# RWKV's core in joint steps of both head pairs, w and a beside attention's end, a gate that overlaps its units: one core, 2432 dense rows

## The reference, cut to what matters

```python
def first_block(x, p, ...):
    h = rmsnorm(x, norm_mix_g[i]);  u = h @ w_in[i]
    u_rwkv, u_attn, u_gate = jnp.split(u, ...)
    o_a = rwkv7_time_mix(u_rwkv, ...)      # 8 heads of 64; w, a, g through small matrices w2, a2, g2
    o_b = diff_attention(u_attn, ...)      # 4 heads, two causal score matrices each, rmsnorm of the output
    g_a, g_b = jnp.split(jax.nn.sigmoid(u_gate), 2, axis=-1)
    merged = g_a * (o_a @ w_proj_a[i]) + g_b * (o_b @ w_proj_b[i])
    x = x + merged @ w_out[i]
    x = x + jnp.square(jax.nn.relu(rmsnorm(x, norm_mlp_g[i]) @ w_ff1[i])) @ w_ff2[i]
    gate = jax.nn.sigmoid(rmsnorm(x, norm_ple_g[i]) @ w_ple_gate[i])
    x = x + (p[i] @ w_ple[i]) * gate       # the first gate of the texts below
    return rmsnorm(x, final_norm_g)
def second_block(x, p, ...):
    # h = rmsnorm(x, ln1) @ w_in: gated linear attention (GLA, 4 heads) and dilated attention
    # (12 heads in 3 groups, mixed by a softmax over the groups' lse), both gated;
    # then w_out, the same MLP, a second gate, the last norm
```

## Time and profile before

| | |
|---|---|
| median of 3 runs | 2204.41 us (2203.53 to 2207.41) |
| profiled execution | 2209.3 us, its span 2207.5 us |
| TensorE busy | 2107.3 us (95%), 11518 matmuls, mean granted clock 0.967 |
| VectorE, ScalarE, GpSimd busy | 979.0 us (44%), 791.4 us (36%), 316.7 us (14%) |
| DMA | 84 GB/s in the mean, 173 MB read from HBM |

### The profile page before, as it was taken

How to read it: one execution, slowest core, us unless ns; L and a number is a source line. 1 busy time by engine, 2 the same in 40 slices (tenths; PEclk the granted TensorE clock), 3 DMA queues, 4 the chain that set the end, 5 groups by cost and what they waited for, 6 DMA issues and landing times.

```text
span 2207.5 us, 27571 instructions
## 1 busy us (share of the span) xinstructions
PE 2107.3 (95%) x11518; PEld 1651.1 (75%) x11518; DVE 979.0 (44%) x1510; ACT 791.4 (36%) x1241; POOL 316.7 (14%) x314
## 2 busy tenths in 40 slices
PE   7889999999999999999889999999899999999996
PEld 5556766767788778888666778888588888888884
DVE  5554454444463233336644344444744442333354
ACT  5445212221445332234642233334332343322344
POOL 2001122121122010012500000000401120100114
PEclk9989998989999999999999999999999999999998
DMA  4112111111442332323231112222132333222221
GB/s 167 48 48 67 49 45 39 46 43 45 148 138 96 105 103 97 100 93 103 94 106 48 48 66 68 81 83 86 48 105 96 99 104 131 96 96 96 96 86 48
DMA packets 59845, 185.47 MB, mean 84 GB/s; under 512 B 6552, under 2 KB 11800, under 8 KB 59593
## 3 DMA queue, kind: packets, MB, share of 16 engines
q1 hardware_dynamic: 59720, 183.71, 24.9%
HBM read 173.46 MB, written 10.22 MB: 83 GB/s over the span
## 4 chain that ended last, share of the span: by engine, by line
PE 85%; DVE 4%; ACT 3%; issue 3%; POOL 3%; DMA 1%; SPq 0%; DVEq 0%; POOLq 0%; ACTq 0%
PE P L493 24%; PE P L495 22%; PE P L494 22%; POOL AREN L2287 1%; POOL AREN L2290 1%; PE P L778 1%; DVE AREN L1615 1%; PE P L794 1%; PE P L787 1%; PE P L845 1%; PE P L844 1%; PE P L933 1%; PE P L735 1%; ACT WHI L1052 1%; PE P L981 1%
## 5 line engine op out<-in xcount | busy, mean ns | idle before, releaser
L493 PE MATMUL P<-HH,WHI 128*128 128x512 f32 x1528 | 651.0, 426 | 19.5 <-DVE WLO L1622 13.9
L495 PE MATMUL P<-HH,WLO 128*128 128x512 f32 x1528 | 608.5, 398 | 0.0
L494 PE MATMUL P<-HL,WHI 128*128 128x512 f32 x1528 | 607.8, 398 | 0.0
L1052 ACT ACTIVATE WHI<-RAW 128x1024 fp32r<-128x1024 f32 x303 | 318.7, 1053 | 395.0 <-PE P L495 392.4
L1622 DVE TENSOR_TENSOR WLO<-RAW,WHI 128x1024 fp32r<-128x1024 f32 x303 | 381.3, 1259 | 155.5 <-ACT WHI L1052 154.1
L493 PEld LDWEIGHTS P<-HH,WHI 128*128 128x128 f32 x1528 | 293.1, 192 | 112.4 <-issue 31.7
L493 PE MATMUL P<-ARR,WHI 128*128 128x512 f32 (+1 forms) x904 | 353.6, 391 | 11.0 <-DVE WLO L1622 7.4
L495 PE MATMUL P<-ARR,WLO 128*128 128x512 f32 (+1 forms) x904 | 352.1, 390 | 0.0
L494 PE MATMUL P<-ARR,WHI 128*128 128x512 f32 (+1 forms) x904 | 352.0, 389 | 0.0
L495 PEld LDWEIGHTS P<-HH,WLO 128*128 128x128 f32 x1528 | 293.8, 192 | 64.8
L494 PEld LDWEIGHTS P<-HL,WHI 128*128 128x128 f32 x1528 | 294.6, 193 | 49.7 <-issue 1.2
(11 more groups left out here) (289 smaller groups left out, 1613.1 us busy)
## 6 DMA issues: line engine op xcount, KB each, us to landing
RAW<-in_w_in_dram SPq DMA_DIRECT2D x118, 512.0 KB, 3.3
RAW<-in_w_ff_dram SPq DMA_DIRECT2D x64, 512.0 KB, 3.3
RAW<-in_w_ml_dram SPq DMA_DIRECT2D x64, 512.0 KB, 3.3
RAW<-in_w_out_dram SPq DMA_DIRECT2D x16, 512.0 KB, 3.3
RAW<-in_w_pg_dram SPq DMA_DIRECT2D x16, 512.0 KB, 3.2
AREN<-in_xT_dram SPq DMA_DIRECT2D x16, 256.0 KB, 6.3
s_gates<-AREN SPq DMA_DIRECT2D x16, 256.0 KB, 2.0
RAW<-in_w_ab_dram SPq DMA_DIRECT2D x8, 512.0 KB, 3.3
```

The costliest lines, as they stand in the source:

```text
L493: e.matmul(out, hi, H[0][:, s], start=first, stop=False)
L494: e.matmul(out, hi, H[1][:, s], start=False, stop=False)
L495: return e.matmul(out, lo, H[0][:, s], start=False, stop=last)
L1052: e.activation(WHI[n % NSPL][:, :], RAW[n % NRAW][:, :], ACT.Copy).then_inc(*D.act.sig("whi", n))
```

## The change

`gate_steps` places the six steps of a unit over two units. `n5` is no longer squared by ScalarE and added by GpSimd: VectorE sums the squares of `n4`, weighted with `GF2` (g_fin squared, formed once). The norm totals stand in rows EMB2 + 8, EMB2 + 14 and HA, and the eight products x by one each in every fourth row of GL.

`attn_steps` lists attention's 64 steps for all engines; several share a row, and `pv` and `ss` of a head stand between the scores of the next one. The steps of w and a (`r`) move from rows 132 to 147 to rows 117 to 131 and into banks 6 and 7. The area of w's and a's results is moved to the end of the buffers, and w2 is loaded into a buffer of pair 1 without a wait; g2 waits for the last head's `bia` (the ALiBi table).

`core_steps` lists 70 steps of a pair: `la` of level 1 also holds the a and v transposes, level 2 the mean, level 4 the variance, level 5 the gate of the quarter before, level 3 the bonus; `lb` holds `lb`, `lc` and in level 5 `x1`; W holds b's transposes, N a state. Each step has its fixed banks. Both pairs take their steps in the same rows, 21 steps of pair 0 ahead, at every second row from 164 on. `yw` and `yb` of GpSimd become two `scalar_tensor_tensor` of VectorE in `result`. Only the last quarter has three steps `E` of its own.

GLA's and the dilated heads' steps share rows (15 steps of a GLA head in 10 rows), the mix takes four rows (HR + 50 to 62) of three steps, with banks 4 to 7.

```diff
 def gate_steps(j, k, n):
 
-    stages = ("evac", "sigmoid", "mult", "add", "hi", "lo")
-    out = [(j, "evac")] if 2 <= j < n and k == 7 else []
-    if j == 2:
-        out = [(i, stages[k - 1 - i]) for i in range(2) if 0 <= k - 1 - i < 6] + out
-    if j > 2 and 1 <= k <= 5:
-        out.append((j - 1, stages[k]))
+
+    out = []
+    for i in range(n):
+        if i == 0:
+            at = (2, 1), (2, 2), (2, 3), (2, 6), (3, 0), (3, 1)
+        elif i == 1:
+            at = (2, 2), (2, 3), (2, 4), (3, 0), (3, 3), (3, 5)
+        elif i < n - 1:
+            at = (i, 7), (i + 1, 1), (i + 1, 2), (i + 1, 6), (i + 2, 0), (i + 2, 1)
+        else:
+            at = (i, 7), (n, 1), (n, 2), (n, 3), (n, 4), (n, 5)
+        out += [(i, what) for what, jk in zip(("evac", "sigmoid", "mult", "add", "hi", "lo"), at) if jk == (j, k)]
     return out
...
+def attn_steps():
+    out = []
+    for h in range(4):
+        out += [("vt", 0, 0)] if h == 0 else []
+        for i in range(8):
+            out += [("pv", h - 1, 0)] if h and i == 1 else [("ss", h - 1, 0)] if h and i == 5 else []
+            out.append(("qk", h, i))
+        out.append(("aw", h, 0))
+        out += [("vt", h + 1, 0)] if h < 3 else []
+        out += [("pt", h, kb) for kb in (3, 2, 1, 0)]
+    out += [("pv", 3, 0), ("ss", 3, 0)]
+    banked = [s for s in out if s[0] != "aw"]
+    return [(*s, (2, 3, 4, 5)[banked.index(s) % 4] if s[0] != "aw" else None) for s in out]
+def core_steps():
+    out = []
+    for q in range(4):
+        out += [("G", q, 0), ("T", q, 0)]
+        for lev in range(1, 6):
+            out += [("la", q, lev), ("lb", q, lev)]
+        out += [("W", q, 0), ("M", q, 0), ("N", q, 0)] + ([("S", q, 0)] if q < 3 else []) + [("O", q, 0)]
+    return out + [("E", 3, i) for i in range(3)]
...
-    def spread(seq, first, last):
-        for i, s in enumerate(seq):
-            at[first + i * (last - first) // len(seq)].append(s)
-
-    for h in range(4):
-        r = (33, 57, 81, 105)[h]
-        put("a", r, *range(r + 3, r + 11), r + 13, *range(r + 17, r + 21), r + 22, r + 24)
-    put("r", 132, *range(136, 144), 147)
-    for jj, first, last in ((0, A_RW + 68, A_GA + 124), (1, A_GA + 4, A_GA + 126)):
-        c, f = f"c{jj}", f"f{jj}"
-        seq = [f, f, f]
-        for q in range(4):
-            more = [f] if q < 3 else []
-            seq += [c] * 8 + more + [c] * 17 + more + [c] * 2 + more + [c] * (5 if q < 3 else 4)
-        spread(seq, first, last)
-    put("n", A_EMB2 + 7, A_EMB2 + 11, A_EMB2 + 13, A_EMB2 + 15)
+    put("a", 32)
+    for r in (39, 62, 85, 108):
+        late = r > 39
+        put("a", r, r, *((r,) if late else ()), r + 2, r + 2, r + 4, r + 4, *((r + 4,) if late else ()), r + 6, r + 6,
+            r + 11, *((r + 12,) if r < 108 else ()), r + 18, r + 18, r + 20, r + 20)
+    put("a", 132, 135)
+    put("r", 117, 119, 119, 122, 122, 125, 125, 128, 128, 131)
+
+    seq = [["f"], ["f"], ["f"]]
+    for what, q, lev in core_steps():
+        seq.append(["c"] + (["f"] if q < 3 and (what in "WN" or (what, lev) == ("la", 3)) else []))
+    n = len(seq)
+    late = [A_GA + 4 + i * 121 // n for i in range(n)]
+    early = list(range(A_RW + 68, A_GA + 2, 2))
+    rest = n - len(early)
+    for i, group in enumerate(seq):
+        put_at = early[i] if i < len(early) else late[(i - len(early)) * (n - 2) // rest]
+        put_steps(at, put_at, group, 0)
+    for i, group in enumerate(seq):
+        put_steps(at, late[i], group, 1)
+    put("n", A_EMB2 + 8, A_EMB2 + 14, A_HA, *range(A_GL + 1, A_GL + 33, 4))
     put("b", A_ML + 80, *range(A_ML + 100, A_ML + 220, 10), A_PG + 24, A_PG + 48, A_HA)
     for h in range(4):
         r = A_GL + 32 * (h + 1) + 1
-        put("g", r, r + 4, r + 5, r + 9, r + 11, *range(r + 13, r + 20), r + 21, r + 23, r + 26)
+        put("g", r, r + 4, r + 4, r + 9, r + 11, r + 13, r + 13, r + 16, r + 16, r + 19, r + 19, r + 22, r + 24, r + 24, r + 27)
     for n in range(12):
         r = A_DL + 33 if n == 0 else A_DL + 24 * (n + 1) + 2
-        put("l", *((r, r + 1, r + 3, r + 7, r + 11, r + 13, r + 16) if n < 4 else (r, r + 1, r + 5, r + 11, r + 16)))
-    put("l", A_HR + 22, A_HR + 23, A_HR + 24, A_HR + 28, A_HR + 33, *range(A_HR + 40, A_HR + 64, 2), A_HR + 66)
+        put("l", *((r, r + 2, r + 2, r + 7, r + 12, r + 12, r + 16) if n < 4 else (r, r, r + 5, r + 11, r + 16)))
+    put("l", A_HR + 20, A_HR + 20, A_HR + 20, A_HR + 27, A_HR + 33, *[A_HR + r for r in (50, 54, 58, 62) for _ in range(3)],
+        A_HR + 67)
...
+        def dil_bank(i):
+            return (2, 3, 4, 5)[i % 4] if i < 56 else (4, 5, 6, 7)[i % 4]
...
-        W2 = v3(bufs[0]["G"][:, 0:512], 4)
+        W2 = v3(bufs[1]["BT"], 4)
...
+                    if what == "la":
+                        o = take(b0, C.dve.at("T", q, lev - 1))
                         for j, p, h in jhp:
                             d = e.matmul(th(o[:, 0:256], j, p, h), Gu(rws[p], j, p, h, 0), th(Tm, j, p, h),
                                          start=True, stop=True)
                         d.then_inc(*C.pe.sig("la", q, lev))
-                        free[b] = C.dve.at("X", q, lev)
-                        yield
+                        free[b0] = C.dve.at("X", q, lev)
+                        if lev == 1:
+                            o = take(b1, *[cc(8 + 2 * jj + j) for j in range(2)])
+                            for j in range(2):
+                                e.transpose(v3(o, 4)[:, j, :], AR[:, j, 0, :, :], ident)
+                            for j, p in jp4:
+                                d = e.matmul(v3(o, 4)[rws[1 - p], 2 + j, :], Vq[:, j, 64 * p:64 * p + 64], ident,
+                                             start=True, stop=True)
+                            d.then_inc(*C.pe.sig("av", q))
+                            free[b1] = C.act.at("vt", q, 1)
+                        if lev == 2 and q:
+                            mean(q - 1, b1)
+                        if lev == 3:
+                            o = take(b1, F.pool.at("rk", q))
+                            e.matmul(o[:, 0:256], cst("bones"), B_["tmp"], start=True, stop=True).then_inc(
+                                *C.pe.sig("bon", q))
+                            free[b1] = C.dve.at("bon", q)
+                        if lev == 4 and q:
+                            variance(q - 1, b1)
+                        if lev == 5 and q:
+                            gate(q - 1, b1)
...
+                            acc, tmps = NORM["n4"]
+                            w.wait_ge(N.act.at("sq", "n4", i), K.pool.at("gf2"), N.dve.at("n5", i - 1))
+                            if i == 0:
+                                e.tensor_scalar(ar(6), ar(acc), GF2[:, 0:1], None, op0=ALU.mult).then_inc(
+                                    *N.dve.sig("n5", 0))
+                            else:
+                                e.scalar_tensor_tensor(out=ar(6), in0=ar(tmps[i % 2]), scalar=GF2[:, i:i + 1],
+                                                       in1=ar(6), op0=ALU.mult, op1=ALU.add).then_inc(
+                                    *N.dve.sig("n5", i))
...
-                w.wait_ge(D.dve.at("rwkv", 1), AT.dve.at("ob", 3))
+                w.wait_ge(D.dve.at("rwkv", 1))
                 e.activation(WA[0:64, :], WA[0:64, :], ACT.Tanh).then_inc(*R.act.sig("tanh"))
                 e.activation(GD, GD, ACT.Sigmoid).then_inc(*R.act.sig("sg"))
...
+                    if what == "la":
                         w.wait_ge(C.pe.at("la", q, lev), C.dve.at("st", 2 * q) if lev == 1 and q else None)
-                        mul(v3(Xm, 4), v3(o[:, 0:256], 4), lb(lev, 4)).then_inc(*C.dve.sig("X", q, lev))
-                        yield
+                        mul(v3(Xm, 4), v3(o0[:, 0:256], 4), lb(lev, 4)).then_inc(*C.dve.sig("X", q, lev))
+                        if lev == 2 and q:
+                            centred(q - 1, o1)
+                        if lev == 3:
+                            w.wait_ge(C.pe.at("bon", q), *[cc(8 + 2 * jj + j) for j in range(2)], C.dve.at("yb", q - 2, 1))
+                            mul(v2[f"bon{q % 2}"], v3(o1[:, 0:256], 2), Vq).then_inc(*C.dve.sig("bon", q))
+                        if lev == 5 and q:
+                            result(q - 1, o1)
...
-                    w.wait_ge(M.act.at("r1"), D.dve.at("HX2", j), N.act.at("sq", "n5", j))
+                    w.wait_ge(M.act.at("r1"), D.dve.at("HX2", j), N.act.at("sq", "n4", j))
                     e.scalar_tensor_tensor(out=ar(XB + j), in0=ar(XB + j), scalar=vec("g_fin", j), in1=R1, op0=ALU.mult,
                                            op1=ALU.mult).then_inc(*M.dve.sig("x", j))
-                yield
+                    yield
...
-                            accumulate("n5", i)
...
-                    w.wait_ge(C.dve.at("yn", q))
-                    mul(v2["W"], v2["W"], col("lnx_w")).then_inc(*C.pool.sig("yw", q))
-                    w.wait_ge(C.pool.at("yw", q), C.pool.at("bon", q))
```

(44 more changed lines are left out.)

764 lines of the change are left out of this document (330 added, 434 removed).

## The result

The changed kernel takes 2121.59 us in the median of four runs (2118.88 to 2124.26) against 2204.03 us, a ratio of 0.9623 (95% interval 0.9606 to 0.9639): 82.4 us faster. 69.3 us were forecast. Between the two profiled executions, whose spans are 2207.5 and 2120.9 us, 86.6 us lie. The sum is nearly met, its terms are not: three parts gave far more than forecast, two less than half.

What follows compares the result with a forecast made beforehand. TensorE was taken as the bound. Attention 18.6, core 11.4, gate 24.5, GLA 5.4, dilated heads 5.4 and mix 4 sum to 69.3 us, for 2135 us; own range 2122 to 2150, whole range 2112 to 2166.

Steps and rivals of the forecast that it cites:

- The unit: All merged side work: each burst merged into another saves TensorE one changeover into side work and back, 0.34 us.
- I count the clock as unchanged: RWKV's core: the output steps, behind which the clock falls, stay eight and never share a burst, so no clock gain.
- a quarter should go: Attention: the lower clock costs 12 us at most, and a quarter of it goes with the waits, 3 us.
- Rival (d): RWKV's core: joint bursts of 64-column matmuls draw the clock down, 73 us lost, 2208 us; chance 0.05.
- Attention: Attention with w and a: fewer bursts, waits gone and clock, less new waits, give 18.6 us (bounds 10 and 29).
- The core's waits: RWKV's core: later fronts 4 us, VectorE standing on ScalarE's copies 4 us, adds behind a weight split 2 us.
- rival (a): Attention and core: the added waits, 10.5 and 10 us, do not come up; 2115 us, chance 0.16.
- The gate: First gate and norms: spreading a unit's chain over two units removes the waits, 24.5 us (bounds 15 and 26).
- rival (c): First gate: VectorE and GpSimd exclude each other, 7.0 us a unit for 5.44, 9 us stay; 2144 us, chance 0.07.
- GLA: GLA: bursts go from 60 to 40, four mergers only lengthen a wait, so 16 x 0.34 = 5.4 us.
- Dilated heads: Dilated heads: bursts go from 56 to 40, worth 5.4 us.
- Mix: The mix: 15 bursts to 5 give 3.4 us; its wait moves to row 48 at 8 us; 4 us in all.

Runs made afterwards that it cites:

- out_split: The changed kernel with each output step cut into two steps of 16 matmuls, at least a dense row between them: 2113.87 us, ratio 0.9581.
- out_pairs: The changed kernel with an output step's 32 matmuls reordered, two with 64-row weights, then two with 128-row weights: 2092.31 us, ratio 0.9524.
- no_attn: The changed kernel with attention's steps and the steps of w and a in their old order and rows: 2148.95 us, ratio 0.9756.
- pool_late: The changed kernel with GpSimd's addition for n4 of units 1 to 5 held back until VectorE's addition of the next unit: 2119.01 us, ratio 0.9652.
- no_gate: The changed kernel with the first gate's part undone, its old places and norm sums back: 2133.65 us, ratio 0.9697.

## Why the prediction was right in its sum and wrong in its terms

- **The unit, 0.34 us a burst: mis-sized, 0.17 where it was measured alone.** I took it from the earlier trace rows as the first side step's price less the second's, but the first is a `la` (L778) and the second an `lb` (L787), two kinds. Moving 31 bursts apart cost 0.17 us each. By stretches, with waits and clock taken off, attention gives 27.0 - 10.2 - 11.7 = 5.1 us for 32 bursts and GLA 13.3 - 6.1 = 7.2 for 15. The core gives 29.7 - 12.7 + 0.6 = 17.6 for 63; at 0.17 the bursts are 10.7 of it, and the rest may be steps that became cheaper beside others; how they share it stays open.
- **The clock: the step that failed.** "I count the clock as unchanged" in the core and "a quarter should go" in attention. It gave 12.7 us in the core, 11.7 in attention, 6.1 in GLA, 30 where 3 were counted; the core's share is the least certain, as the same core's clock differs from trace to trace. Rival (d) did not happen: with joint bursts the core's clock rose from 0.92 to 0.95. `out_split` and `out_pairs` show that what draws it down there is the output step, with its 4.1 us of slow matmuls in one piece. In attention the waits are the likely cause, though no run sets them apart: in the kernel before six of its windows at the lower clock begin 2.4 to 3.8 us after the start of a wait of 1.5 or 2.5 us, and with the old steps the clock was back at 0.94 in `no_attn`.
- **Attention: 27.0 for 18.6.** Its waits of 15.2 us went, and 5.0 came in place of 10.5: 1.8 on the tanh (3.6 forecast), 2.6 at row 134 (1.5), 0.6 at `pv` in row 107, none on the weighted scores, where 5.4 were forecast. VectorE was not late there.
- **The core's waits: wrong.** L752 waits 11.2 us over 8, 1.4 each as before, where 1.9 each were forecast, 4 us more in all ("still over 11" could not tell the two apart); the others are 5.4 us in all, against 5.0 before. The 10 us that I added did not come, which is rival (a)'s half.
- **The gate: 11.1 for 24.5.** VectorE's unit was counted with 0.75 us for the weighted sum and took 1.78 in all seven, beside GpSimd's addition: 0.75 + 1.79 + 2.31 + 0.68 + 0.68 = 6.2 us for 5.44. That is rival (c)'s mechanism, put at 0.07, but `pool_late`, which takes it from five of the seven sums, wins only 2.5 us. The larger error is in the sum: I put all of the stretch's 26.6 lost us down to waits that would go, while its row has TensorE standing for 90.56 - 74.38 = 16.2 us, and the other 10 are the clock (0.89). Of the standing, 8.8 us are left: 4.5 on evacuations, most of it (2.9) in row 1062, 2.5 on weights and 1.2 on a norm total. By the Trainium skill ("SBUF — State Buffer", Who interferes with whom) the two exclude each other and whoever issues first holds the ports; the trace agrees, with 1.79 us beside the addition and 0.74 without. I gave the rule too small a chance because one row of 0.75 seemed to speak neither way.
- **GLA: 13.3 for 5.4**, 6.1 of it the clock, which in part was the old gate's doing (`no_gate`). **Dilated heads: 2.9 for 5.4**: 20 bursts at 0.15, the last GLA head's among them. **Mix: right in its wait.** It was forecast to move to an evacuation at row HR + 48 with 8 us, and is 7.7 us there; the stretch gained 1.8 us for 4, as its clock fell from 0.95 to 0.90 (3.3 us).
- **What the errors did together.** The unit took away some 9 us over all parts, the gate 13 and the clock in HR 3; the clock elsewhere gave 27 more than counted and the waits that did not come another 15: 17 us net, the distance from 69.3 to 86.6. The median is 13 us below the forecast and inside the whole range, but just outside the forecast's own (2122 to 2150), between it and rival (a)'s 2115. That the sum came so near is luck in good part, and the profiled gain of 86.6 us is not evidence for the terms.

## What to carry to other kernels

Price a changeover from two bursts that differ in nothing else, never from steps of two kinds. Where the granted clock is below 1, a wait or a slow stretch that goes can be worth more than its length, so put a term for it, and compare the clock of unedited stretches before a gain is put down to an edit. Before a stretch's lost time is put down to waits, take its busy time from its length. And before spreading steps, look at each step's own matmuls: one reordering of an output step's 32 gave 22 to 31 us, a quarter to a third of what the whole change gave.

## What the runs showed of the hardware

- Float32 matmuls with 64 columns of weights, two in the trace for each of the program's, took 0.26 us for one of the program's where 64-row and 128-row weights alternated, and the same 0.26 us for two of it where two of one shape, on different halves of the output, followed one another.
- VectorE's sum of two tiles in SBUF took 1.79 us beside GpSimd's addition and 0.74 without; GpSimd's product took 1.58 us when VectorE began second and 2.06 when VectorE began first.
- The granted clock fell to its lower level within 5 us of the start of four of the eight output steps of 4.1 us in the changed kernel's core, though TensorE did not stand there; with steps of 2.1 us behind none.
